# A gated unit laid over three groups of 384 tokens, and modulation products spread over four strips of 32 partitions

## The reference, cut to what matters

```python
mod = jax.nn.silu(cond) @ lp['w_ada'] + lp['b_ada']
sh1, sc1, g1, sh2, sc2, g2 = jnp.split(mod[:, None, :], N_MOD, axis=-1)
h = rms_norm(x, lp['norm1_g']) * (1.0 + sc1) + sh1
```

```python
y = jax.nn.gelu(y)
y = y * jax.nn.sigmoid(y @ w_glu.astype(f32) + b_glu.astype(f32))
```

## Time and profile before

| | us |
|---|---|
| median of 3 runs | 2169.68 |
| lowest and highest | 2169.28, 2173.42 |
| profiled execution | 2169.53 |
| its span, first to last instruction | 2167.7 |

### The profile page before, as it was taken

The page is one execution under the profiler, slowest core; times in us unless marked ns, Lnnn a source line. Parts: engine busy times, 40 slices in busy tenths (PEclk is TensorE's granted clock), DMA queues, the critical chain, the costliest instruction groups (busy, mean ns, idle before and its releaser), DMA issues. The chain is left out here.

```text
span 2167.7 us, 55496 instructions
## 1 busy us (share of the span) xinstructions
PE 1842.1 (85%) x24160; PEld 1149.9 (53%) x24160; DVE 1038.4 (48%) x1685; ACT 633.9 (29%) x1233; POOL 524.9 (24%) x596
## 2 busy tenths in 40 slices
PE   6289577789999468999988379799999999999988
PEld 1234476335555258888888244355545455554533
DVE  8789566420888724555545644332221222212276
ACT  0511244322555323444444213231112121120202
POOL 0510000232111024555544433231202121120110
PEclk9589699889999779999999679899999999999999
DMA  6574332511344443333343222211111121111122
GB/s 232 218 210 174 122 110 80 182 43 41 118 151 152 140 156 96 105 103 101 95 143 91 100 100 98 107 57 60 40 39 40 39 78 39 40 39 39 40 74 92
DMA packets 172362, 215.87 MB, mean 100 GB/s; under 512 B 41035, under 2 KB 127051, under 8 KB 170447
## 3 DMA queue, kind: packets, MB, share of 16 engines
q1 hardware_dynamic: 172244, 214.18, 29.9%
HBM read 151.63 MB, written 60.42 MB: 98 GB/s over the span
## 5 line engine op out<-in xcount | busy, mean ns | idle before, releaser
L89 PE MATMUL psum<-arena 128*128 128x384 bf16 (+1 forms) x2028 | 711.5, 351 | 71.2 <-PEq L500 14.7
L90 PE MATMUL psum<-arena 128*128 128x384 bf16 (+1 forms) x2028 | 710.9, 351 | 0.0
L91 PE MATMUL psum<-arena 128*128 128x384 bf16 (+1 forms) x2028 | 710.2, 350 | 0.0
L1625 PE MATMUL psum<-arena 64*64 64x64 f32 x9216 | 347.5, 224 | 39.2 <-issue 32.6
L89 PEld LDWEIGHTS psum<-arena 128*128 128x128 bf16 x2028 | 201.1, 99 | 267.5 <-issue 41.2
L1625 PEld LDWEIGHTS psum<-arena 64*64 64x64 f32 x9216 | 312.4, 136 | 56.4 <-issue 51.3
L1619 PE MATMUL psum<-arena 64*64 64x64 f32 (+2 forms) x6336 | 286.5, 238 | 56.6 <-DMA arena<-xrec 38.5
L91 PEld LDWEIGHTS psum<-arena 128*128 128x128 bf16 x2028 | 201.3, 99 | 178.9 <-issue 9.0
L90 PEld LDWEIGHTS psum<-arena 128*128 128x128 bf16 x2028 | 201.3, 99 | 171.8 <-issue 7.6
L1619 PEld LDWEIGHTS psum<-arena 64*64 64x64 f32 x6336 | 245.5, 135 | 63.5 <-issue 60.8
L1752 ACT ACTIVATE arena<-psum 128x192 f32<-128x192 f32 (+2 forms) x624 | 173.3, 334 | 293.5 <-PE psum L1625 186.8
(11 more groups left out here) (274 smaller groups left out, 2006.2 us busy)
## 6 DMA issues: line engine op xcount, KB each, us to landing
arena<-in_w_ff SPq DMA_DIRECT2D x16, 2048.0 KB, 7.8
arena<-in_w_ada SPq DMA_DIRECT2D x12, 2048.0 KB, 8.4
arena<-xrec SPq DMA_DIRECT2D x72, 320.0 KB, 3.3
arena<-s_tab SPq DMA_DIRECT2D x8, 1600.0 KB, 7.4
x<-arena SPq DMA_DIRECT2D x18, 512.0 KB, 2.6
xrec<-arena SPq DMA_DIRECT2D x4, 2304.0 KB
...
```

Of the source, the lines that this page charges most:

```text
L89: nc.tensor.matmul(out, whi, xhi, start=first, stop=False)
L90: nc.tensor.matmul(out, wlo, xhi, start=False, stop=False)
L91: return nc.tensor.matmul(out, whi, xlo, start=False, stop=last)
L1625: done = nc.tensor.matmul(out[half[1 - h]], lhs[half[h]], rhs[half[h]], start=first, stop=last)
```

## The change

**Modulation.** The stationary operand `M.silu` grows from two columns to 32 (30 of them zero), and the eight matmuls of a piece write four strips of 32 partitions of the bank in turn (k mod 4), two per strip; the bias goes into strip 0. `keep_row` copies all 128 partitions. The four partial sums are added by a matmul with `M.strips`, a 128 x 2 matrix with a one in each strip: `turn` uses it in place of the transpose, and a new `gate` does it for the rows that stay rows, two fp32 matmuls of 512 columns, followed by a new ACT copy `keep_gate`, on which the DMA of the gates now waits. The front stage gets a memset of `M.silu` and a `reduce_sum` for `M.strips` on DVE.

**Gated unit.** The work is laid over three groups of 384 tokens (three turns each) for all four channel blocks at once, so that every elementwise instruction handles 1536 elements a partition in place of 1152, in three groups in place of four. Within a group the tokens stay in the order of the turns, so DVE's copy out (`evict`) has no step; the step of 8 is now in `keep` (ACT) and `keep_low` (POOL), which write the result back in natural order. `products` 0 to 3 stand between the groups' products. The factor 0.5 of gelu is moved into the constants behind it, which removes one DVE instruction per group. The context rows are loaded first.

```diff
-        nc, out = self.nc, self.M.ps[0:2, self.banks[i % 2], :]
+        nc, ps, bank = self.nc, self.M.ps, self.banks[i % 2]
         need(pe, self.ev("ada_row"), i - 1)
         if i == 0:
             pe.wait_ge(self.ev("ada_bias"), 16)
-        nc.tensor.matmul(out, self.M.ident[0:2, 0:2], self.rows[0:2, i * 512:(i + 1) * 512], start=True, stop=False)
+        nc.tensor.matmul(ps[0:32, bank, :], self.M.ident[0:2, 0:32], self.rows[0:2, i * 512:(i + 1) * 512], start=True, stop=False)
         pe.wait_ge(self.ev("ada_w", i % 2), 16 * (i // 2) + 16)
         for k in range(KD):
-            last = nc.tensor.matmul(out, self.M.silu[:, k, :], self.wst[i % 2][:, k, :], start=False, stop=(k == KD - 1))
+            c = k % 4
+            last = nc.tensor.matmul(ps[32 * c:32 * c + 32, bank, :], self.M.silu[:, k, :], self.wst[i % 2][:, k, :],
+                                    start=(0 < k < 4), stop=(k >= 4))
...
-        self.nc.scalar.activation(self.rows[0:2, i * 512:(i + 1) * 512], self.M.ps[0:2, self.banks[i % 2], :], ACT.Copy)\
+        self.nc.scalar.activation(self.rows[:, i * 512:(i + 1) * 512], self.M.ps[:, self.banks[i % 2], :], ACT.Copy)\
...
-            last = self.nc.tensor.transpose(self.M.ps[:, bank, at + 2 * k:at + 2 * k + 2],
-                                            self.rows[0:2, half * D + k * P:half * D + (k + 1) * P], self.M.ident[0:2, 0:2])
+            last = self.nc.tensor.matmul(self.M.ps[:, bank, at + 2 * k:at + 2 * k + 2],
+                                         self.rows[:, half * D + k * P:half * D + (k + 1) * P], self.M.strips, start=True, stop=True)
         last.then_inc(self.ev("cols"), 1)
+
+    def gate(self, pe, half, bank):
+        pe.wait_ge(self.ev("ada_row"), 2 * half + 2)
+        for q in range(2):
+            last = self.nc.tensor.matmul(self.M.ps[0:2, bank + q, :], self.M.strips, self.rows[:, half * D + q * 512:half * D + q * 512 + 512],
+                                         start=True, stop=True)
+        last.then_inc(self.ev("gate_sum"), 1)
+
+    def keep_gate(self, act, half, bank):
+        act.wait_ge(self.ev("gate_sum"), 1)
+        self.nc.scalar.activation(self.rows[0:2, half * D:half * D + D].rearrange("p (q n) -> p q n", q=2), self.M.ps[0:2, bank:bank + 2, :], ACT.Copy)\
+            .then_inc(self.ev("gate_row"), 1)
...
+            op(nc.vector.memset(M.silu, 0.0))
...
+            nc.vector.reduce_sum(M.strips, M.ident.rearrange("p (c x) -> p x c", x=32)[:, 0:2], mybir.AxisListType.X).then_inc(ev("strips"), 1)
...
-            sp.wait_ge(ev("ada_row"), 2)
+            sp.wait_ge(ev("gate_row"), 1)
...
+            mod.keep_gate(act, 0, 0)
...
+            mod.gate(pe, 0, 0)
...
+    def natural(v, g):
+
+        lat = v[:, :, 0:NLAT].rearrange("p k (c t) -> p k t c", t=CH)
+        return [(lat[:, :, 3 * g:min(3 * g + 3, CH)], slice(0, min(3, CH - 3 * g) * P))] + ([(v[:, :, NLAT:T].unsqueeze(2), slice(2 * P, TW))] if g == 2 else [])
...
+            sp.dma_start(y_nat, ins["y_bounce"]).then_inc(ev("ctx"), 16)
             sp.dma_start(wst, ins["w_glu"]).then_inc(ev("w"), 16)
             sp.dma_start(bias, ins["b_glu"]).then_inc(ev("w"), 16)
-            sp.dma_start(y_nat, ins["y_bounce"]).then_inc(ev("ctx"), 16)
...
-            sp.wait_ge(ev("turned"), CH)
+            sp.wait_ge(ev("turned"), TG)
...
+            def turn(g):
+                need(pe, ev("turned_read"), g)
+                if g == TG - 1:
                     pe.wait_ge(ev("ctx"), 16)
...
+                for n in range(3):
+                    t = 3 * g + n
+                    for k in range(K4):
+                        src = M.y_lat[:, t, k * P:(k + 1) * P] if t < CH else y_nat[:, k * P:(k + 1) * P]
+                        last = nc.tensor.transpose(ps[:, n, k * P:(k + 1) * P], src, M.ident)
                 last.then_inc(ev("turned"), 1)
+
+            def product(g):
+                pe.wait_ge(ev("y_lo"), g + 1)
+                if g == 0:
+                    pe.wait_ge(ev("w_lo"), 1)
+                for o in range(K4):
+                    n = K4 * g + o
+                    need(pe, ev("tanh_z"), n - 2)
+                    for k in range(K4):
+                        last = split_mm(nc, ps[:, 3 + n % 3, 0:TW], whi[:, k, o * P:(o + 1) * P],
+                                        wlo[:, k, o * P:(o + 1) * P], yhi[g % 2][:, k], ylo[g % 2][:, k], k == 0, k == K4 - 1)
+                    last.then_inc(ev("z"), 1)
+            for g in range(TG):
+                turn(g)
             mod.products(pe, 0)
+            product(0)
             mod.products(pe, 1)
+            product(1)
             mod.products(pe, 2)
...
+            product(2)
             mod.products(pe, 3)
-            mod.turn(pe, 0, 6, 0)
+            mod.turn(pe, 0, 2, 0)
+            mod.gate(pe, 1, 0)
...
+            def evict(g):
+                dve.wait_ge(ev("turned"), g + 1)
+                need(dve, ev("gelu"), g - 1)
+                nc.vector.tensor_copy(banks(yt[g % 2]), ps[:, 0:3, :].rearrange("p t (k c) -> p t k c", k=K4)).then_inc(ev("turned_read"), 1)
+
+            def cubic(g):
+                dve.wait_ge(ev("square"), g + 1)
+                c.step(nc.vector.tensor_scalar(g1[g], g1[g], 0.044715, 1.0, ALU.mult, ALU.add))
+                c.settle(dve)
+                nc.vector.tensor_tensor(g1[g], g1[g], yt[g % 2], ALU.mult).then_inc(ev("cubic"), 1)
+
+            def gelu(g):
+                dve.wait_ge(ev("tanh"), g + 1)
+                nc.vector.scalar_tensor_tensor(out=g1[g], in0=g1[g], scalar=1.0, in1=yt[g % 2], op0=ALU.add, op1=ALU.mult).then_inc(ev("gelu"), 1)
+
+            def out(g):
+                v = g2[g % 2]
+                dve.wait_ge(ev("tanh_z"), K4 * g + K4)
+                c.step(nc.vector.tensor_scalar(v, v, 0.25, 0.25, ALU.mult, ALU.add))
+                c.settle(dve)
+                dve.wait_ge(ev("gelu"), g + 1)
+                nc.vector.tensor_tensor(v, v, g1[g], ALU.mult).then_inc(ev("out"), 1)
+            evict(0)
...
+            evict(1)
+            cubic(0)
+            gelu(0)
+            evict(2)
+            cubic(1)
+            gelu(1)
+            cubic(2)
+            out(0)
+            gelu(2)
+            out(1)
+            out(2)
...
+            def square(g):
+                act.wait_ge(ev("turned_read"), g + 1)
+                nc.scalar.activation(g1[g], yt[g % 2], ACT.Square).then_inc(ev("square"), 1)
+
+            def tanh(g):
+                act.wait_ge(ev("cubic"), g + 1)
+                nc.scalar.activation(g1[g], g1[g], ACT.Tanh, scale=math.sqrt(2 / math.pi)).then_inc(ev("tanh"), 1)
+
+            def high(g):
+                act.wait_ge(ev("gelu"), g + 1)
+                need(act, ev("z"), K4 * (g - 1))
+                nc.scalar.activation(yhi[g % 2], g1[g], ACT.Copy).then_inc(ev("y_hi"), 1)
+
+            def gates(g):
+                if g == 0:
+                    act.wait_ge(ev("bias"), 1)
+                need(act, ev("out_lo"), g - 1)
+                for o in range(K4):
+                    n = K4 * g + o
+                    act.wait_ge(ev("z"), n + 1)
+                    nc.scalar.activation(g2[g % 2][:, o], ps[:, 3 + n % 3, 0:TW], ACT.Tanh, bias=bias[:, o:o + 1], scale=0.25).then_inc(ev("tanh_z"), 1)
+
+            def keep(g):
+                act.wait_ge(ev("out"), g + 1)
+                for dst, cols in natural(M.ys_hi, g):
+                    src = g2[g % 2][:, :, cols].rearrange("p k (t c) -> p k t c", c=P)
+                    nc.scalar.activation(dst, src, ACT.Copy).then_inc(ev("out_hi"), 1)
+            square(0)
             act.wait_ge(ev("w"), 32)
...
+            tanh(0)
+            square(1)
+            high(0)
+            tanh(1)
+            mod.keep_row(act, 0)
+            high(1)
+            square(2)
+            gates(0)
+            tanh(2)
+            mod.keep_row(act, 1)
+            high(2)
+            keep(0)
+            gates(1)
             mod.keep_row(act, 2)
...
+            keep(1)
+            gates(2)
+            keep(2)
             mod.keep_row(act, 3)
+            mod.keep_gate(act, 1, 0)
...
+            def low(g):
+                pool.wait_ge(ev("y_hi"), g + 1)
+                need(pool, ev("z"), K4 * (g - 1))
+                nc.gpsimd.tensor_tensor(ylo[g % 2], g1[g], yhi[g % 2], ALU.subtract).then_inc(ev("y_lo"), 1)
+
+            def keep_low(g):
+                pool.wait_ge(ev("out_hi"), g + 1 + (g == 2))
+                for (dst, cols), (hi, _) in zip(natural(M.ys_lo, g), natural(M.ys_hi, g)):
+                    src = g2[g % 2][:, :, cols].rearrange("p k (t c) -> p k t c", c=P)
+                    nc.gpsimd.tensor_tensor(dst, src, hi, ALU.subtract).then_inc(ev("out_lo"), 1)
             pool.wait_ge(ev("w_hi"), 1)
...
+            low(0)
+            low(1)
+            low(2)
+            keep_low(0)
+            keep_low(1)
+            keep_low(2)
```

89 lines of the change are left out of this document (14 added, 75 removed).

## The result

The changed kernel is slower. Its median is 2185.76 us in 6 runs (2181.63 to 2191.58) against 2170.39 us for the kernel before in 6 runs on the same chip; the ratio of the means is 1.0066, with a 95% interval of 1.0047 to 1.0085. The forecast was 2162.7 us with a range up to 2169.0, so it has the wrong sign and the range doesn't hold the time. The profiled execution of the changed kernel took 2183.18 us.

What follows compares the result with a forecast made beforehand. Each stage's last wait bounds the kernel: DVE in front and u, PE's phases in the gated unit. Gated unit -7.1, front +0.3, u 0: -6.8 from 2169.53 gives 2162.7 us; own range 2160.5 to 2165.3, overall 2157.0 to 2169.0.

Steps and rivals of the forecast that it cites:

- the price of the stepped copies: Gated unit: `keep` on ACT 1.5 us (factor 1.0, bound 1.6), `keep_low` on POOL 4.05 us (factor 1.3, bound 1.58).
- rival 1: Gated unit: stepped copies dear, DVE held off, PE at half clock before `gate`; stage -4.1 or -2.2 us; chance 0.2.
- Front: Front stage: the added memset and small reduction lengthen DVE's chain, +0.3 us; PE's shorter pieces gain nothing.
- u: Stage u: DVE's queue gets nothing new and ends the stage, so the change in time is 0.
- A piece: Modulation piece on PE: four strips run side by side, so piece with bias takes 2.9 us.
- Rivals 3 and 4: Modulation pieces: no strip overlap, 8.0 us each, 2175.1 us, chance 0.1; or two strips at once, 4.5 us, 2165.2, chance 0.08.
- DVE held off by POOL: Gated unit: DVE instructions with all inputs in SBUF wait each time until POOL's instruction ends; 3.8 us at the start.
- Rival 2: Gated unit: DVE is not held off by POOL, so those waits go; stage -12.3 us, 2157.5 us; chance 0.12.
- First low half: Gated unit, first group: weights split by 407.4, then cubic, tanh, gelu, high half and POOL's 3.1 us low half, ending at 417.2.
- Product 0 and piece 1: PE in the gated unit: first product takes 10.7 us plus 1 us wait, ending at 428.8; then the 2.9 us piece.
- End of the stage: Gated unit's close: row 3's copy, `gate` 1.9 us, `keep_gate` 1.05, then 2.7 to the next stage, at 463.5.
- The rule on POOL of the Trainium skill: Gated unit: reads with steps over 8 bytes cost more; `keep_low` factor 1.5, 4.7 us, stage ending 0.9 us later.

Runs made afterwards that it cites:

- the ladder: Changed kernel plus a measuring stage: each engine alone writes or reads 1536 elements a partition at steps 1 to 8; ACT's bf16 write took 1.48 to 7.00 us.
- experiment 3: Changed kernel with `keep` and `keep_low` writing tokens in group order, without the step, and later stages taking that order; 2163.36 us, ratio 0.9961.
- experiment 1: Kernel before with only the new modulation (four strips, `gate`, `keep_gate`) and the old gated unit; 2171.86 us, ratio 1.0003.
- experiment 7: Changed kernel with POOL's low half written packed, ACT's copy left stepped (later results differ); 2183.03 us, ratio 1.005.
- experiment 6: Changed kernel with ACT's high half written packed, POOL's write left stepped (later results differ); 2173.22 us, ratio 1.0007.
- 8: Kernel of experiment 3 with POOL's low half of the weights waiting for the first cubic and row 3's copy ahead of the last `keep`; 2162.8 us, ratio 0.996.
- 15: Kernel of experiment 3 with the same two waits moved and the strip matrix given 64 bytes of a partition instead of 8; 2163.32 us, ratio 0.996.

## Why the prediction was wrong

**The step that failed** is the size of one term, the price of the stepped copies. The prediction took `keep` at 1.5 us with an upper bound of 2.4, and `keep_low` at 4.05 with a bound of some 4.9; they took 7.0 and 7.1. That is the sign that the prediction itself had named, `keep_low` over 5 us. The bounds came from L635 on DVE, f32 in and out, and the factor was carried over from an f32 read on DVE to bf16 writes on two other engines, as if type and direction didn't matter. On the ladder no single factor serves even for f32 written with a step of 8 (1.67 on DVE, 2.0 on ACT, 1.01 on POOL); for bf16 the upper bound of `keep` is three times too low. No row of before gave an upper end for such a write, and the text should have left the term open above and put more than 0.2 on rival 1. Rival 1 (dear copies) named the mechanism and its consequences, DVE held off, PE idle before `gate` and the half clock there, all of which the trace shows; its price was -2.2 us for the stage at most where +11.4 came. By its own terms, twice 0.9 us on POOL and 1.9 us of half clock, the first of its two sums comes to -3.4 and not -4.1, which changes nothing.

**The rest of the sum held.** With the step taken out (experiment 3) the kernel took 2163.36 us against the 2162.7 forecast, and the stage 68.4 against 70.6. That the totals agree so well is in part luck: the stage was 2.2 us shorter than the sum, and RWKV and close, which the sum left as they were, took 926.7 us instead of 922.9. Point by point:

- *Front* +0.3: the last DVE instruction starts at 61.58 instead of 61.19, the stage is 62.8 instead of 62.3 us. Right.

```profile
61.58 0.16 DVE L380 SCALAR_TENSOR_TENSOR arena<-psum,arena 128x16 f32<-128x16 f32 x1
```

- *u* 0: 111.5 us against 111.1, ended by the table entries as before. SP issues the gates at 224.70, behind the stores.
- *A piece* 2.9 us: L145 1.04 and L149 1.92 (experiment 1, and 429.74 above). Four strips of 32 run side by side, eight matmuls in 1.9 us instead of 7.04. The Trainium skill's 2.38 for three strips ("TensorE: Matmul & The Clock Gate", Part 3) scaled to 3.2 us for a piece; the trace gives 7.04 / 1.92 = 3.7 for four. Rivals 3 and 4 fall.
- *DVE held off by POOL*: right everywhere it was used, and somewhat dearer, since DVE ends 0.8 us after POOL. Rival 2 falls.
- *First low half* at 24.3 us of the stage: 414.48 + 2.90 - 394.91 = 22.5. The weights were split by 406.96, 12.1 us into the stage, where 14.5 was allowed for; the bound from L937's issue was too careful, as that DMA's issue takes 0.34 us when it stands first (L962 at 394.91).
- *Product 0 and piece 1*: piece 1 begins at 428.77, 33.9 us in, forecast 35.9, again early by 2 us. Up to here the changed kernel ran ahead of the forecast. From the first `keep` on (436.17) it fell behind.
- *End of the stage* by row 3, `gate` and `keep_gate`: right, 475.08 to 480.34, with `gate` at half clock.
- *The rule on POOL of the Trainium skill* ("GPSIMD Engine Reference", Performance pitfalls for Q7 kernels) spoke against the layout, and rightly. It is about reads, and for the read alone its factor of 1.5 is near: in experiment 7, POOL reads with the step and writes without, 4.20 us against 2.90, which is 1.45, and on the ladder it is 4.18 against 3.11, 1.34. The write, which it doesn't name, makes it 7.0, also where POOL reads packed (7.09 in experiment 6).

One statement ahead of the prediction is wrong, though nothing in the sum rests on it: most of PE's busy time is not the MLP's, which has 754 of 1842 us.

**What stays open.** Of the 15.4 us between the medians 11.4 are the stage's, and -1.0 lies ahead of it. Some 3 us in RWKV and close are there in three profiles of each kernel. In the kernels with the new modulation, with any gated unit, this part took 922.4 to 927.9 us (eleven profiles), without it 920.1 to 924.9 (five); its code and addresses are the same in all but experiments 3, 8 and 15. The difference lies in the recurrence, 455.0 to 459.2 us in the eleven and 451.5 to 456.6 in the five, at nearly the same granted clock (0.963 and 0.964 in the mean). No run tells what carries over from one to the other, and the 8 bytes were ruled out.
